# Gate steps spread over the 32 items of an expert-activation part: 24 in a row, or three of every four

## The reference

```
experts = e1 * 128 + e2                    # 128 chosen experts per token, with gates
a = einsum('td,tkd->tk', hb, take(w_u, ib))     # one activation per token and choice
c = gb * gelu(a)                                # gb: the gates
y = einsum('tk,tkd->td', c, take(w_v, ib))
```

## Time and profile before

| what | value |
|---|---|
| median of 3 runs | 2915.59 us (2904.64 to 2915.82) |
| the profiled execution | 2914.41 us, its span 2912.6 us, mean granted clock 0.988 |
| PE busy | 2781.1 us, 95% of the span |
| DVE busy | 2129.5 us, 73% |
| ACT busy | 1340.1 us, 46% |
| DMA | 692.34 MB, mean 238 GB/s |
| U1 (PE) | about 1778 to 1971.5 us |
| V0 (PE) | 1971.5 to about 2126 us |

### The profile page before, as it was taken

How to read it: one execution, slowest core, us unless ns; L and a number is a source line. 1 busy time by engine, 2 the same in 40 slices (tenths; PEclk the granted TensorE clock), 3 DMA queues, 4 the chain that set the end, 5 groups by cost and what they waited for, 6 DMA issues and landing times.

```text
span 2912.6 us, 39271 instructions
## 1 busy us (share of the span) xinstructions
PE 2781.1 (95%) x15570; PEld 2423.3 (83%) x15570; DVE 2129.5 (73%) x2671; ACT 1340.1 (46%) x1504; POOL 204.9 (7%) x141
## 2 busy tenths in 40 slices
PE   7999979899999899999989999999999999999998
PEld 6888868779888788887889999997789878987776
DVE  4656766554678654546566999978989888988898
ACT  4544454444344443334553554454444444444444
POOL 0000000000000000000000000001211111123232
PEclk9999999999999999999999999999999999999999
DMA  6554544245545355544435555669999999999997
GB/s 240 186 206 174 184 143 172 72 162 170 178 159 187 109 182 179 190 158 157 175 134 171 198 201 197 237 252 363 390 358 374 369 402 348 368 344 382 364 387 289
DMA packets 113061, 692.34 MB, mean 238 GB/s; under 512 B 12904, under 2 KB 25952, under 8 KB 34416
## 3 DMA queue, kind: packets, MB, share of 16 engines
q1 hardware_dynamic: 73152, 522.03, 49.0%
q0 software_dynamic: 18832, 136.88, 11.9%
q10 hardware_dynamic: 20960, 31.84, 3.1%
HBM read 676.45 MB, written 13.63 MB: 237 GB/s over the span
## 4 chain that ended last, share of the span: by engine, by line
PE 66%; DVE 17%; DMA 8%; ACT 6%; ACTq 2%; issue 2%; DVEq 0%; SPq 0%
PE ps L802 9%; PE ps L804 9%; PE ps L803 9%; DVE w_lo L2166 9%; DMA raw<-in_w_v 5%; PE ps L1264 5%; ACT w_hi L1408 4%; PE ps L860 3%; PE ps L862 3%; PE ps L861 3%; PE ps L1267 3%; PE ps L1312 3%; PE ps L1318 2%; PE ps L1314 2%; PE ps L1317 2%; PE ps L1313 2%
## 5 line engine op out<-in xcount | busy, mean ns | idle before, releaser
L2166 DVE TENSOR_TENSOR w_lo<-raw,w_hi 128x2048 fp32r<-128x2048 f32 (+2 forms) x500 | 1128.3, 2261 | 422.5 <-ACT w_hi L1408 416.0
L1408 ACT ACTIVATE w_hi<-raw 128x2048 fp32r<-128x2048 f32 (+2 forms) x500 | 943.3, 1893 | 777.6 <-DMA raw<-in_w_v 325.6
L802 PE MATMUL ps<-w_hi,hT 128*128 128x512 f32 (+3 forms) x1344 | 520.4, 387 | 12.1 <-DVE w_lo L2166 11.6
L804 PE MATMUL ps<-w_hi,hT 128*128 128x512 f32 (+3 forms) x1344 | 513.3, 382 | 0.0
L803 PE MATMUL ps<-w_lo,hT 128*128 128x512 f32 (+3 forms) x1344 | 512.8, 382 | 0.0
L1264 PE MATMUL ps<-hT,w_hi 128*128 128x384 f32 x1536 | 415.4, 352 | 11.6 <-DVE w_lo L2166 8.3
L802 PEld LDWEIGHTS ps<-w_hi,hT 128*128 128x128 f32 x1344 | 253.9, 189 | 59.4 <-DVE w_lo L2166 8.5
L804 PEld LDWEIGHTS ps<-w_hi,hT 128*128 128x128 f32 x1344 | 253.7, 189 | 45.9
L803 PEld LDWEIGHTS ps<-w_lo,hT 128*128 128x128 f32 x1344 | 254.1, 189 | 44.4
L1267 PEld LDWEIGHTS ps<-hT,w_lo 128*128 128x128 f32 x1536 | 278.1, 188 | 0.0
L1267 PE MATMUL ps<-hT,w_lo 128*128 128x192 f32 x1536 | 277.9, 262 | 0.0
(11 more groups left out here) (334 smaller groups left out, 4547.7 us busy)
## 6 DMA issues: line engine op xcount, KB each, us to landing
raw<-in_w_u_t SPq DMA_DIRECT2D x128, 1024.0 KB, 5.5
raw<-in_w_v SPq DMA_DIRECT2D x128, 1024.0 KB, 8.8
raw<-in_w_in_2.0 SPq DMA_DIRECT2D x32, 1024.0 KB, 4.8
raw<-in_odd_w.0 SPq DMA_DIRECT2D x20, 1024.0 KB, 4.7
raw<-in_even_w.3608 SPq DMA_DIRECT2D x16, 1024.0 KB, 4.8
raw<-in_w_out.0 SPq DMA_DIRECT2D x16, 1024.0 KB, 4.8
raw<-in_w_out.1 SPq DMA_DIRECT2D x16, 1024.0 KB, 4.8
raw<-in_w_out_2.0 SPq DMA_DIRECT2D x16, 1024.0 KB, 4.8
```

What stands on the lines that cost most here:

```text
L802: pe.matmul(o, hi, wh, start=(j + k == 0), stop=False)
L804: mm = pe.matmul(o, lo, wh, start=False, stop=(j == 3 and k == 3))
L1408: act.activation(w_hi[:, s, 0:size], raw[:, s, 0:size], ACT.Copy).then_inc(hi_done, 1)
L2166: dve.tensor_tensor(w_lo[:, s, 0:size], raw[:, s, 0:size], w_hi[:, s, 0:size].bitcast(F32), ALU.subtract).then_inc(lo_done, 1)
```

## The change

Step g moves from item g to item 4 (g // 3) + g % 3: the items 3, 7, 11, ..., 31 have none, and the last step stands beside item 30. On PE the two loops over U1 become one over four pairs of rounds, 8 items each. ACT's loop likewise has 8 items in its body and runs three times; the last 8 items are written out.

```
@@ PE
-        def dense(i, s):
-            pe.wait_ge(rows_ready, 4 * i + n)
+        def dense(i, g):
+            pe.wait_ge(rows_ready, 6 * i + n)
...
-        with pe.Fori(0, STEPS // RAW) as i:
-            for s in range(RAW):
-                activations(i, s, 1)
-                dense(i, s)
-        with pe.Fori(STEPS // RAW, LOOPS) as i:
-            for s in range(RAW):
-                activations(i, s, 1)
+        with pe.Fori(0, LOOPS // 2) as i:
+            for r in range(2 * RAW):
+                activations(2 * i + r // RAW, r % RAW, 1)
+                if r % RAW < 3:
+                    dense(i, 3 * (r // RAW) + r % RAW)
@@ ACT
-            act.wait_ge(gates_out[s % 2], 32 * i + 16 * (s // 2 + 1))
+            act.wait_ge(gates_out[s % 2], 48 * i + 16 * (s // 2 + 1))
...
-                with act.Fori(0, STEPS // RAW) as i:
+                with act.Fori(0, LOOPS // 2 - 1) as i:
+                    for r in range(2 * RAW):
+                        u_split(2 * i + r // RAW, r % RAW, q)
+                        activate(2 * i + r // RAW, r % RAW, q)
+                        if r % RAW < 3:
+                            keep(i, 3 * (r // RAW) + r % RAW)
+                for s in range(RAW):
+                    u_split(LOOPS - 2, s, q)
+                    activate(LOOPS - 2, s, q)
+                    if s < 3:
+                        keep(LOOPS // 2 - 1, s)
...
                 activate(LOOPS - 1, s, q)
+                if q == 1 and s < 3:
+                    keep(LOOPS // 2 - 1, 3 + s)
@@ DVE
-                if m + 1 < STEPS:
-                    hots(m + 1)
+                g = 3 * i + s
+                if s < 3 and g + 1 < STEPS:
+                    hots(g + 1)
...
                 add_halves(i, s, 1)
                 u_split(i, s, 1)
-                if m < STEPS:
-                    weigh(i, s)
+                if s < 3:
+                    weigh(g // 4, g % 4)
```

More of the change, by code:

```diff
@@ L1278, in activations @@
             mm.then_inc(item_used, 1)
-        def dense(i, s):
-            n = s + 1
-            b = s % 2
-            pe.wait_ge(rows_ready, 4 * i + n)
-            pe.wait_ge(hot_ready, 4 * i + n)
-            pe.wait_ge(kept, 4 * i + n)
+        def dense(i, g):
+            n = g + 1
+            b = g % 2
+            pe.wait_ge(rows_ready, 6 * i + n)
+            pe.wait_ge(hot_ready, 6 * i + n)
+            pe.wait_ge(kept, 6 * i + n)
             for k in range(TG):
@@ L1979, in keep @@
         def keep(i, s):
-            act.wait_ge(gate_used, 4 * i + (s + 3))
-            act.wait_ge(gates_out[s % 2], 32 * i + 16 * (s // 2 + 1))
+            act.wait_ge(gate_used, 6 * i + (s + 3))
+            act.wait_ge(gates_out[s % 2], 48 * i + 16 * (s // 2 + 1))
             act.activation(STAGE[:, s % 2].rearrange("p (e t) -> p e t", t=TG),
@@ L1985, in keep @@
                            ACT.Copy).then_inc(kept, 1)
-            act.wait_ge(kept, 4 * i + (s + 3))
-            act.dma_start(gates_kept[:, :, bass.ds(4 * i + s, 1)].rearrange("p q a x -> p (q a) x"),
+            act.wait_ge(kept, 6 * i + (s + 3))
+            act.dma_start(gates_kept[:, :, bass.ds(6 * i + s, 1)].rearrange("p q a x -> p (q a) x"),
                           STAGE[:, s % 2].rearrange("p (q x) -> p q x", q=KEPT)).then_inc(gates_out[s % 2], 16)
@@ L2012, in u_part @@
             if q == 1:
-                with act.Fori(0, STEPS // RAW) as i:
+                with act.Fori(0, LOOPS // 2 - 1) as i:
[9 more added lines that the diff above has]
+                        keep(LOOPS // 2 - 1, s)
+            else:
+                with act.Fori(0, LOOPS - 1) as i:
                     for s in range(RAW):
@@ L2016, in u_part @@
                         activate(i, s, q)
[L2017 to L2021, removed]
             for s in range(RAW):
```

## The result

| | before | changed |
|---|---|---|
| median | 2912.77 us (2904.64 to 2918.68, 10 runs) | 2923.07 us (2916.95 to 2926.62, 10 runs) |
| ratio | | 1.0033, 95% interval 1.0021 to 1.0045 |
| profiled execution, span | 2914.41, 2912.6 us | 2924.42, 2922.6 us |
| U1, first matmul to V0's first | 193.5 us | 200.7 us |
| V0 | 160.7 us | 162.8 us |

The loss is clear of the uncertainty. (Such lengths are read from the starts of PE's first matmuls of each part in the profiled executions. V0 runs here to U2's first matmul, at 2132.3 us before, where the table of the kernel before says about 2126. In the two profiled executions of the changed kernel, this one and one of a later run, U1 agrees within 0.1 us, V0 differs by 1.5 us and V1 by 3.4 us, so the 0.7 us of the last row say nothing, and the 2.1 us of V0 little.)

The account below looks back on a forecast made before the run. PE was taken to bound U1 first, then a ring of waits through ACT and DVE, with DMA saturated behind U1. A gain of 6.9 us less 1.9 for gathers and border gave -5.0, so 2910 us; range 2901 to 2919.

Parts of the forecast that it names:

- What bounds U1: In U1, PE sets the early rounds at 6.014 us; from step 12 a slower chain of waits does, 6.35 us.
- the lead: In U1, splits are two items ahead of PE when steps begin; some 0.3 us an item is used up.
- the ring: U1's dependence chain through ACT and DVE: high split, low split, `weigh`, `keep`, gate DMA; 6.35 us a round.
- the sum has 6.9: PE's whole loss from step 2 to V0's first matmul, 6.9 us, which the spread was to remove; bounds 5.5 to 6.9.
- for the item without a step DVE's sum and split, 0.56 + 2.29 us ... 21.9 us: In U1, four items need 21.9 us on the chain of waits, under PE's 22.6, so lag is regained at the fourth.
- PE waits 1.4 to 1.5 us: At the end of U1, the last step beside item 30 makes PE wait 1.4 to 1.5 us for V0's operands.
- The late gathers: POOL's gathers 1 and 2 start about 2.5 us into V0 and delay its weights by 1.9 us; bounds 1.4 to 6.7.
- Rival A: In V0, late gathers take the gain and stall DVE's first gathered rows 6.0 us: 2920.2 us; chance 0.10.
- Rival B: U1 stays as it is, perhaps lagging inside each group of three; only the moves cost: 2916.3 us; chance 0.13.
- Rival C: V0 takes the gathers in its room and makes up the border's 1.4 us: 2907.5 us; chance 0.12.
- Rival D: PE's longer U1 loop, 400 matmuls, exposes instruction fetches at its three jumps back: 2914.5 to 2929.8 us; chance 0.10.
- the dear end of D: Four exposed instruction fetches per jump back of PE's U1 loop, 20.4 us, giving 2929.8 us.

Follow-up runs that it names:

- Cutting the ring in the kernel before: Kernel before with ACT's high split ahead of `keep`: ratio 0.9978, repeated 0.9977; or with gate DMAs issued by SP instead of ACT: 0.9982.
- with spread steps and no loss left in U1: Changed kernel with ACT's high split for the next item ahead of `keep` all over U1: 0.9995, repeated 0.9994 against the kernel before.
- the run on the end of U1: Changed kernel with the high split of V0's item 1 and its first two operands' casts ahead of the last `keep` on ACT: 2919.76 us, ratio 1.0029.

## Why the prediction was wrong

- **What bounds U1** was right, and so was its size: PE at 6.01 us a round until the lead is used up, then the ring. Cutting the ring in the kernel before took U1 from 193.5 to between 186.6 and 187.1 us in four profiled executions, a gain of 6.4 to 6.9 us where the sum has 6.9. (Of the 3.9 us of waits that the prediction sets beside the 3.7 us behind the last step only 3.0 us come there, the two of 1.5 us; the other 0.9 lie in the slow rounds. The sum doesn't use them.)
- **"for the item without a step DVE's sum and split, 0.56 + 2.29 us ... 21.9 us"** is the step that failed, and with it the gain of 6.9 us in U1, which was a loss of 7.2. It took the fourth round for sum and split alone. But a round of the ring runs from one low split to the next, and what stands there on DVE is what the code puts between them: the order of the changed kernel has the three table instructions behind the fourth split, ahead of the next sum. The round is 5.55 us, the group 24.3 instead of 21.9, above PE's 22.6. The lag of 1.7 us a group uses the lead up in two groups instead of twelve items. The order of the changed kernel on DVE, on record ahead of the prediction, has the tables in that place. With only these tables ahead of the split the groups were at 22.6 us, so this is shown and not only read from a timeline.
- **"PE waits 1.4 to 1.5 us" at the border**: the count from item 30 took DVE and ACT as level with PE. The last `weigh` began at T + 6.7 (1973.52 - 1966.80) and not at T + 2.8. Those 3.9 us of lag and the 1.4 come to 5.3 us, near the 5.15 measured. Most of it is the same error once more: with the tables moved the wait was 2.3 us. The other 0.9 us is about the lag that three rounds of the ring gather within the last group, 0.7 us, which the count from item 30 left out though the prediction names it. In the kernel before, the eight items without a step stood at the end and repaid the lag before V0.
- **The late gathers**, 1.9 us: 0.07 and 0.08%, or 2.0 and 2.3 us, in two comparisons whose uncertainty takes in nothing as well, so the size is borne out but not shown. They started 2.3 us into V0, where 2.5 was forecast:

```profile
1980.46 1.39 POOL L2150 DMA_INDIRECT work<-in_w_u_rows,gsm  x1 [196.51 <-DMA gates_kept<-work]
```

  By the Trainium skill ("Trainium Kernel Development and Optimization", Key Constraints), DMAs issued from SP, ACT and POOL run on the same 16 engines and interleave. The trace agrees: in the kernel before with held gathers the share in V0's first 13 us rose from 0.74 to 0.91, so the gathers found room there, as the prediction had it.
- **Rival A** had the right side and the wrong place: 7.2 us of the loss are in U1. DVE used row 1 at 1995.39 us, 17.3 us into V0, with no wait before it:

```profile
1995.39 2.29 DVE L3028 CUSTOM_DVE_ANT_0 work<-work 128x2048 f32<-128x2048 f32 x1
```

- **Rival B** had part of the mechanism ("it lags inside each group of three") and priced it as no gain, when the group was longer than before. **Rival C**, that V0 takes the gathers and the border's wait for nothing, is not what the runs suggest: with spread steps and no loss left in U1 the gain was 0.05 and 0.06%, 1.5 and 1.7 us, where U1 was 7.0 and 5.8 us shorter. **Rival D** was wrong: with 400 matmuls in PE's loop the instruction queue q8 moved 3 packets over U1, as before, and with the ring cut all its groups, over the three jumps back, are 10.60, 6.01 and 6.01 us. By the Trainium skill ("Runtime: NRT & Kernel Launch", Instruction fetch mechanics) a taken branch out of the current window of two pages forces a fetch; no cost of it shows at this size of loop.
- **The range** ended at 2919 us, near rival A. But for the dear end of D, no term or rival let U1 become longer, because all took the fourth item as repaying at least what the group loses. The time of 2923.07 us near A's 2920.2 is chance: A has no part in it.

## What to carry to other kernels

Where two engines wait for each other around a ring, count a round as everything that stands between the same instruction and its next occurrence on each engine, the free item's round too, and compare the sum over the pattern with the bound engine's. Idle time spread evenly helps only if the work in the free slot stands ahead of what the ring waits for; otherwise it is better bunched where it repays the lag before the next border. Here cutting the ring was better than moving work: one ACT instruction ahead of another brought U1 what the spread was to bring, and the whole time 0.22 and 0.23%.

## What the runs showed of the hardware beside it

After PE's wait of 5.15 us at V0's start its granted clock was 0.77 on average over the next 7 us. Its first matmuls of 512 columns were 0.43 us apart and then, from 1981.22 us on, 0.23 us: first 1.2 GHz and then 2.4. That cost 1.5 us over the first eight. Busy time by stretch of the changed kernel, against the earlier trace rows:

```profile
1972.00:1985.00 13.00, 7.85 (x32) 6.42 (x31) 8.74 (x14) 8.18 (x10) 4.24 (x2) 0.87 0.68 213
...
1978.00:1985.00 7.00, 6.88 (x24) 5.62 (x25) 6.40 (x11) 4.96 (x6) 4.24 (x2) 0.77 0.64 186
```

After the wait of 2.45 us in the run on the end of U1 the clock stayed at 1.00.
